# Attention inside a transformer layer: projections and value products cut in pieces and moved to other steps

## The reference, cut to what matters

```python
def diff_attention(q, k, v, lam):
    ...
    def block(qi):                     # 128 queries
        s = jnp.einsum('bqhtd,bkhtd->bhtqk', qi, k).astype(jnp.float32)
        p = jax.nn.softmax(s, axis=-1)
        a = p[:, :, 0] - lam * p[:, :, 1]
        return jnp.einsum('bhqk,bkhe->bqhe', a.astype(v.dtype), v)

h = rms_norm(x, g_pre_mix[l]) * (1.0 + sc1) + sh1
p = h @ w_in[l]
q, k, v, z, gates = jnp.split(p, SPLITS, axis=-1)
q = partial_rope(q.reshape(B, S, ATTN_HEADS, 2, ATTN_HEAD_DIM), cos, sin)
k = partial_rope(k.reshape(B, S, ATTN_HEADS, 2, ATTN_HEAD_DIM), cos, sin)
o = diff_attention(q, k, v, lam)
```

## Time and profile before

| | |
|---|---|
| median of three runs | 5690.43 us (5686.27 to 5692.12) |
| span of the profiled execution | 5687.6 us |
| PE busy / weight loads | 5157.5 us (91%) / 4000.4 us (70%) |
| DVE, ACT, POOL busy | 2979.1 (52%), 1455.1 (26%), 152.1 us (3%) |
| mean granted clock of TensorE | 0.905 of full speed |

### The profile page before, as it was taken

How to read it: one execution, slowest core, us unless ns; L and a number is a source line. 1 busy time by engine, 2 the same in 40 slices (tenths; PEclk the granted TensorE clock), 3 DMA queues, 4 the chain that set the end, 5 groups by cost and what they waited for, 6 DMA issues and landing times. The chain is left out here.

```text
span 5687.6 us, 59986 instructions
## 1 busy us (share of the span) xinstructions
PE 5157.5 (91%) x21520; PEld 4000.4 (70%) x21520; DVE 2979.1 (52%) x4767; ACT 1455.1 (26%) x1603; POOL 152.1 (3%) x96
## 2 busy tenths in 40 slices
PE   2999988869888789999999699999999999999997
PEld 2666655657666666666666478888888888888885
DVE  5676762145333685555555377744444444444445
ACT  3444442132212213333333211111111211111111
POOL 0000000010000000010001000000000000000000
PEclk9999987979898888788777699999999999999998
DMA  3000001134321101333333343422222222222212
GB/s 117 19 24 21 24 10 48 52 133 168 110 81 74 52 22 52 104 110 102 110 102 104 109 148 146 147 74 73 75 73 66 77 77 67 66 77 77 66 66 78
DMA packets 236046, 455.34 MB, mean 80 GB/s; under 512 B 12320, under 2 KB 143776, under 8 KB 232736
## 3 DMA queue, kind: packets, MB, share of 16 engines
q1 hardware_dynamic: 218656, 386.75, 20.4%
q10 hardware_dynamic: 11520, 37.75, 1.7%
q0 software_dynamic: 5760, 29.36, 1.5%
HBM read 336.38 MB, written 117.44 MB: 80 GB/s over the span
## 5 line engine op out<-in xcount | busy, mean ns | idle before, releaser
L2016 DVE TENSOR_TENSOR y<-y,psum 128x512 f32<-128x512 f32 x1024 | 680.4, 685 | 374.6 <-PE psum L375 374.4
L373 PE MATMUL psum<-act_hi,v_hi 128*128 128x512 f32 x2048 | 800.1, 391 | 55.2 <-DVE v_lo L1993 52.3
L374 PE MATMUL psum<-act_lo,v_hi 128*128 128x512 f32 x2048 | 798.8, 390 | 0.0
L375 PE MATMUL psum<-act_hi,v_lo 128*128 128x512 f32 x2048 | 798.6, 390 | 0.0
L373 PE MATMUL psum<-in_hi,u_hi 128*128 128x512 f32 x1408 | 548.0, 389 | 1.9 <-DVE u_lo L1982 1.9
L374 PE MATMUL psum<-in_lo,u_hi 128*128 128x512 f32 x1408 | 547.9, 389 | 0.0
L375 PE MATMUL psum<-in_hi,u_lo 128*128 128x512 f32 x1408 | 547.9, 389 | 0.0
L1986 DVE SCALAR_TENSOR_TENSOR g<-g,psum 128x1024 f32<-128x1024 f32 x88 | 107.5, 1222 | 769.9 <-ACT psum L1951 769.9
L373 PEld LDWEIGHTS psum<-act_hi,v_hi 128*128 128x128 f32 x2048 | 385.5, 188 | 139.9 <-issue 52.8
L1951 ACT ACTIVATE psum<-psum 128x1024 f32<-128x1024 f32 x88 | 88.7, 1008 | 1513.0 <-PE psum L375 1513.0
L375 PEld LDWEIGHTS psum<-act_hi,v_lo 128*128 128x128 f32 x2048 | 385.5, 188 | 80.3
(11 more groups left out here) (332 smaller groups left out, 8371.2 us busy)
## 6 DMA issues: line engine op xcount, KB each, us to landing
route_scratch<-sc_stage SPq DMA_DIRECT2D x32, 2048.0 KB, 10.7
g<-route_scratch SPq DMA_DIRECT2D x128, 512.0 KB, 3.3
v_raw<-peer_v_dram SPq DMA_DIRECT2D x128, 512.0 KB, 5.1
u_raw<-peer_uT_dram SPq DMA_DIRECT2D x88, 512.0 KB, 5.3
sc_u_raw<-peer_uT_dram SPq DMA_DIRECT2D x42, 512.0 KB, 5.3
hidden_scratch<-sc_gelu_t ACTq DMA_DIRECT2D x40, 512.0 KB, 6.2
u_raw<-hidden_scratch SPq DMA_DIRECT2D x40, 512.0 KB, 4.4
gates_ada<-w_adaT_dram POOLq DMA_DIRECT2D x16, 1024.0 KB, 5.7
```

The lines of the kernel that those rows point to most:

```text
L373: pe.matmul(out, w_hi, x_hi, start=start, stop=False)
L374: pe.matmul(out, w_hi, x_lo, start=False, stop=False)
L375: return pe.matmul(out, w_lo, x_hi, start=False, stop=stop)
L2016: dve.tensor_tensor(to, to, ps[:, 4 + n % 4], ALU.add).then_inc(added, 1)
```

## The change

Four things change in the attention's programs, and no instruction of the arithmetic is added or removed:

- `project` and `times_v` are returned as pieces; each step runs four eighths of its block of 24 matmuls ahead of `turn`, and four behind it.
- `PROJECTS` moves to steps 1, 2, 3, 5, 6, 7, `times_v(h, 1)` to step 0 of the next head. Each step of a head has now one block of 24.
- `scores` is called apart for map 0 and map 1, with `prepare` between them. `PREPARES` moves to steps 2, 3, 4, 6, 7, and the last value half (`LAST_V`) to step 0 of its own head. `SPLITS` moves to 0, 3, 6.
- ACT and DVE follow: in steps 0 and 4 `turned_hi` comes behind the exponentials, `out` behind it; on DVE `swing` or `low` of values comes ahead of `combine`. The first two and the last two heads are written out, the rest is the loop.

The diff, cut to its core: the loop and the tables, the bodies of ACT and DVE, then PE's program.

```diff
@@ -592,17 +595,20 @@
 
             def all_heads(eng, body, first=None):
 
-                with eng.Fori(0, HEADS // 2 - 1) as it:
+                body(None, Head(0, 0), Head(0, 1))
+                body(Head(0, 0), Head(0, 1), Head(0, 2))
+                with eng.Fori(1, HEADS // 2 - 1) as it:
                     for c2 in range(2):
-                        body(Head(it, c2), Head(it, c2 + 1))
+                        body(Head(it, c2 - 1), Head(it, c2), Head(it, c2 + 1))
                 last = HEADS // 2 - 1
-                body(Head(last, 0), Head(last, 1))
-                body(Head(last, 1), None)
-
-
-            PROJECTS = {b: b for b in range(6)}
-            PREPARES = {b: b - 1 for b in range(1, 7)}
-            SPLITS = {0: (QQ, 0), 2: (VV, 0), 4: (KK, 1)}
+                body(Head(last, -1), Head(last, 0), Head(last, 1))
+                body(Head(last, 0), Head(last, 1), None)
+            PROJECTS = {1: 0, 2: 1, 3: 2, 5: 3, 6: 4, 7: 5}
+            PREPARES = {2: 0, 3: 1, 4: 2, 6: 3, 7: 4}
+            LAST_V = 5
+            SPLITS = {0: (QQ, 0), 3: (VV, 0), 6: (KK, 1)}
 
...
-                    def body(h, g):
+                    def body(before, h, g):
                         for b in range(BPH):
                             e = PREPARES.get(b)
+                            if b == 0:
+                                high(h, LAST_V)
                             if g and e is not None and HALVES[e][0] == VV:
                                 high(g, e)
-                            turned_hi(h, b)
+                            if b % 4:
+                                turned_hi(h, b)
                             if b + 1 < BPH:
                                 exps(h, b + 1)
                             elif g:
                                 exps(g, 0)
+                            if b % 4 == 0:
+                                turned_hi(h, b)
+                                if b:
+                                    out(h, 0)
+                                elif before:
+                                    out(before, 1)
                             if g and b in SPLITS:
                                 i, after = SPLITS[b]
                                 if not after:
@@ -691,11 +707,8 @@
                                     split_weights(g.next(), i)
                             if g and e is not None and HALVES[e][0] != VV:
                                 high(g, e)
-                            if b == 4:
-                                out(h, 0)
                             if g and b in PROJECTS:
                                 copy(g, PROJECTS[b])
-                        out(h, 1)
...
-                    def body(h, g):
+                    def body(before, h, g):
                         for b in range(BPH):
-                            combine(h, b)
                             e = PREPARES.get(b) if g else None
+                            if b == 0:
+                                low(h, LAST_V)
                             if e is not None:
                                 if HALVES[e][0] == VV:
                                     low(g, e)
                                 else:
                                     swing(g, e)
+                            combine(h, b)
                             if b + 1 < BPH:
                                 maxima(h, b + 1)
...
-                        for k in range(KT):
+                        def piece(k):
                             last = self.product3(pe, job, w_hi[:, r, k], w_lo[:, r, k], h_hi[:, k, cols(half)], h_lo[:, k, cols(half)],
                                                  k == 0, k == KT - 1)
-                        last.then_inc(projected, 1)
+                            if k == KT - 1:
+                                last.then_inc(projected, 1)
+                        return piece
 
                     def prepare(g, e):
                         i, half = HALVES[e]
@@ -848,20 +869,22 @@
                             last = pe.matmul(job, self.rotate[:], plain[:, e % 2], start=True, stop=True)
                         last.then_inc(prepared, 1)
 
-                    def scores(h, b):
+                    def scores(h, b, m):
                         q = slice(b * P, (b + 1) * P)
-                        if b == 0:
+                        own = map_rows[m]
+                        if m == 0 and b == 0:
+                            pe.wait_ge(x_split, h.at(6, 9))
+                        if m == 0 and b == BPH // 2:
 
                             pe.wait_ge(x_split, h.at(6, 10))
-                        for m in range(2):
-                            own = map_rows[m]
-
-                            pe.wait_ge(exped, h.at(2 * BPH, 2 * b + m + 1))
-                            for half in range(2):
-                                to = ps[:, 2 * m + half]
-                                pe.matmul(to, q_twice[:, h.par, m, q], k_both[:, h.par, m, cols(half)], start=True, stop=False)
-                                last = pe.matmul(to, q_lo[own, h.par, q], k_both[own, h.par, m, cols(half)], start=False, stop=True)
-                            last.then_inc(scored, 1)
+                        pe.wait_ge(exped, h.at(2 * BPH, 2 * b + m + 1))
+                        for half in range(2):
+                            to = ps[:, 2 * m + half]
+                            pe.matmul(to, q_twice[:, h.par, m, q], k_both[:, h.par, m, cols(half)], start=True, stop=False)
+                            last = pe.matmul(to, q_lo[own, h.par, q], k_both[own, h.par, m, cols(half)], start=False, stop=True)
+                        last.then_inc(scored, 1)
 
...
-                        for k in range(TB):
+                        def piece(k):
                             v = slice(k * P, (k + 1) * P)
                             last = self.product3(pe, o_acc, v_hi[:, h.par, v], v_lo[:, h.par, v],
                                                  a_hi[:, k], a_lo[:, k], k == 0, k == TB - 1)
-                        last.then_inc(out_summed, 1)
-
-                    def body(h, g):
+                            if k == TB - 1:
+                                last.then_inc(out_summed, 1)
+                        return piece
+                    def body(before, h, g):
                         for b in range(BPH):
-                            if b + 1 < BPH:
-                                scores(h, b + 1)
-                            elif g:
-                                scores(g, 0)
+                            coming = (h, b + 1) if b + 1 < BPH else (g, 0) if g else None
+                            if coming:
+                                scores(*coming, 0)
+                            if b == 0:
+                                prepare(h, LAST_V)
                             if g and b in PREPARES:
                                 prepare(g, PREPARES[b])
+                            if coming:
+                                scores(*coming, 1)
+                            piece = None
                             if b == 4:
-                                times_v(h, 0)
+                                piece = times_v(h, 0)
+                            elif b == 0 and before:
+                                piece = times_v(before, 1)
+                            elif g and b in PROJECTS:
+                                piece = project(g, PROJECTS[b])
+                            for k in range(0, 4):
+                                if piece:
+                                    piece(k)
                             turn(h, b)
-                            if g and b in PROJECTS:
-                                project(g, PROJECTS[b])
-                            if b == BPH - 1:
-                                times_v(h, 1)
+                            for k in range(4, KT):
+                                if piece:
+                                    piece(k)
                     first = Head(0, 0)
                     for e in range(6):
-                        project(first, e)
-                        prepare(first, e)
-                    scores(first, 0)
+                        piece = project(first, e)
+                        for k in range(KT):
+                            piece(k)
+                        if e != LAST_V:
+                            prepare(first, e)
+                    for m in range(2):
+                        scores(first, 0, m)
                     all_heads(pe, body)
+                    piece = times_v(Head(HEADS // 2 - 1, 1), 1)
+                    for k in range(KT):
+                        piece(k)
 
```

More of the change, by code:

```diff
@@ L583, in next, with before @@
                     return Head(self.it, self.c + 1)
+                def before(self):
+                    return Head(self.it, self.c - 1)
                 def ring(self, i):
@@ L707, in _ @@
                             split_weights(first.next(), KK)
-                        high(first, e)
+                        if e != LAST_V:
```

(5 more changed lines are left out.)

## The result

The changed kernel is slower: a median of 5735.68 us over four runs (5729.82 to 5740.09) against 5688.35 (5680.82 to 5692.12) in four runs of the kernel before, a ratio of 1.008 with a 95% interval of 1.0066 to 1.0095. Forecast were 5755 us and a range of 5705 to 5795. The profiled span is 5728.2 us against 5687.6, 40.6 more.

A forecast was written before the change was run, and what follows sets the result against it. PE was taken to bound the kernel: 83.7 us of work, 12.9 of waits and 9.9 of clock a head. Seven heads make 745.5 against 668.8, +76.7, less 12 at the ends: 5755 us, range 5705 to 5795.

The forecast's parts named there:

- The chains of ACT and DVE: PE waits for ACT's and DVE's queues in steps 1, 3, 4, 5, 7: 1.6, 1.4, 2.1, 4.5, 3.3 us.
- The sum of the waits: PE's five new waits in each head together: 12.9 us.
- The work: PE's work in a head without any wait, including 0.7 us for divided blocks: 83.7 us.
- The clock: Slower PE clock after waits: 1.5 us for each of three short, 2.7 for each of two long; 9.9 a head.
- The ends: Outside the seven heads: 8 us less in head 0's step 0, 4 less in the last head; 12 less.
- The rival of the long waits only: Only PE's two long waits a head slow the clock, 5.4 us a head: +33, 5724 us; chance 0.12.
- The other side: PE's waits don't arise and blocks fill all eight steps: 83.7 us a head, 5595 us; chance 0.07.

The follow-up runs named there:

- experiment 1: Changed kernel with DVE taking combine of the next step ahead of turned_lo in steps 0 and 4: 5691.77 us, ratio 0.9998 to the kernel before.
- experiment 2: Changed kernel with ACT's copy of a projection ahead of split and high instead of behind them: 5691.56 us, ratio 0.9999 to the kernel before.
- experiment 4: Changed kernel with ACT's copy first, DVE's combine early and low of keys and queries later, value half 4 transposed into o_acc: 5580.0 us, ratio 0.9802.
- experiment 5: experiment 4 without the division: all eight pieces of a block stand behind turn; 5573.3 us, ratio 0.9804 to the kernel before.
- experiment 9: experiment 4 with ACT's copies of steps 2 and 3 last again, two short waits a step apart: 5646.39 us, ratio 0.992.
- experiment 8: experiment 4 with ACT's copy of step 2 alone last again, one short wait: 5609.98 us, ratio 0.9867 to the kernel before.
- experiment 7: experiment 4 with value half 4 back in job and low ahead of the maxima in step 7, one long wait: 5622.64 us, ratio 0.9892.
- experiment 3: Changed kernel without the division: all eight pieces of a block stand behind turn; 5842.89 us, ratio 1.0265 to the kernel before.
- experiment 10: experiment 3 with DVE taking combine ahead of swing and low of values: 5717.23 us, ratio 1.0044 to the kernel before.
- experiment 6: Changed kernel with the edits of experiment 1 and experiment 2 together: 5657.88 us, ratio 0.9952 to the kernel before.

## Why the prediction was right, and where its sizes were off

**The chains of ACT and DVE: right.** Predicted were five waits of 1.6, 1.4, 2.1, 4.5 and 3.3 us in steps 1, 3, 4, 5 and 7; measured are 0.7 to 1.1, 1.38, 1.89, 4.2 and 3.03. Experiments 1 and 2 show the two causes the steps named: the order on DVE for steps 1 and 5, the copy behind split and high on ACT for 3, 4 and 7. The queues were followed row by row, and in steps 3, 4, 5 and 7 the errors are 0.0 to 0.3 us.

**The sum of the waits: 12.9 forecast, 10.8 measured.** Step 1 was taken worst, 0.5 to 0.9 too long. Its chain counted 0.27 us from PE's start to ACT's; in step 5 it was 0.20 (626.15 to 626.35). PE also reached `turn` later, since scores and half a block took 6.32 us, not 6.08. That covers about 0.3 us; the rest of its error stays open. The errors of the other four steps add 0.8. The last part is step 5 in heads 2 and 5: there the trace has the clock low just before, PE came to `turn` later and waited 2.6 instead of 4.2. In experiment 2, where the clock is not low there, step 5 waits 4.2 us in all six heads. A low clock hides part of the next wait, and the sum had added both in full.

**The work: 83.7 forecast, 82.6 measured** (experiment 4). The term that was too large is the rotation, taken at 1.1 us: in experiment 5 a step takes 4.17 us from its first scores matmul to `turn` with a rotation and 3.31 without, 0.86 for each of the four.

**The clock: 9.9 us a head forecast, 8.5 measured**, the busy time of the six heads over that of experiment 4 (546.81 less 495.71, by six). That it came so near is partly luck, for the forecast's prices, 1.5 for a short wait and 2.7 for a long one, fail elsewhere: the two short waits of experiment 9 should cost 3.0 and cost 5.7, the three waits of experiment 1 should cost 5.7 and cost 9.1 (550.34 less 495.71, by six). By experiment 8 a short wait has an average price of 4/6 x 3.1 = 2.1. The five waits of the changed kernel come at 1.7 each, the two of experiment 9 at 2.8, the three of experiment 1 at 3.0. So no price per wait holds for all orders, and why five cost less than three was not tried. The clock fell more often than before, but not as often as the forecast said: 19 low stretches in the six heads, about three a head and not four or five, against 10 in the kernel before. From experiment 8, 12.29 us of extra busy time over 6 x 4.6 us of low clock, each us of low clock costs 0.45. With it, a head is 82.6 plus idle time plus 0.45 x low clock: 95.8 before (14.2 us low; measured 95.8), 101.6 after (measured 101.9), 98.0 in experiment 1 (98.4), 96.0 in experiment 2 (96.3). With the 3.04 us wait of experiment 7 it gives 0.5 too much, 89.1 for 88.6, and with the waits of 4 to 7 us in experiments 3 and 10 it gives 2.8 and 2.7 too much (from 82.0 of work: 122.3 for 119.5, 105.0 for 102.3). There part of the low stretch lies in the idle time, where it costs nothing: the clock is 0.84 in the wait of experiment 7 shown above, and 0.61 in the 7.13 us wait of the same head in experiment 10.

**The ends: 12 forecast, 11 measured** (6.6 and 4.5).

So the chain of waits held, and three terms were too large in the same direction: work by 1.1 us a head, waits by 2.1, clock by 1.4, in all 4.6 (106.5 forecast, 101.9 measured). They didn't cancel one another. Over the seven heads, head 0 being slower than the other six, it was 27.8 us (745.5 against 717.7). Forecast were +65, measured are +41 by the spans and +47 by the medians.

**The rival of the long waits only.** The Trainium skill (TensorE: Matmul & The Clock Gate, HAM oscillation) ties drops to long idle gaps. Taken so that 1.4 to 2.1 us pass free it does not hold here: 1.38 us alone had a drop in four of six heads. The total could not have told, since the 5724 us of this rival lie nearer to the measured 5736 than the forecast's 5755. A later section of the same page (A second HAM failure mode: psum-queue depth-cycling), which the prediction had not weighed, says of a kernel that goes round its PSUM banks in each iteration that short idle times between groups of matmuls, if frequent enough, make the clock swing too; in experiments 8 and 9 one and two short waits a head were enough for drops. The waits of 1.0 us and below that stand in experiments 2 and 6 beside longer ones were not tried alone; whether they ever lower the clock stays open.

**The other side.** The Trainium skill (Perfetto Trace Analysis, Optimization Strategy) says that interleaving stretches of different limits can help. Here it does once ACT and DVE are ordered for it: with every step of a head holding one block, experiments 4 and 5 leave 0.02 us of idle time a head and less and gain 2% (5580.0 us in experiment 4, where this rival had 5595). For this change it was put low, and it did not come. Its condition had two parts, waits below 8 us a head and a clock that holds. Experiment 1 met the first (6.7 us) and not the second, and came out no faster than the kernel before.

## What to carry to other kernels

When the pacing engine's blocks are spread evenly, walk each helper's queue in program order from the event that starts it to the one that the pacing engine asks for; each chain that had slack from a long block is now late by what the block lost. Put the instruction that the pacing engine asks for first ahead of any that waits for another engine (here `combine` ahead of `low`, `copy` ahead of `high`), and only then decide whether blocks need dividing: with the queues right, whole blocks did as well. Remove the waits to the last one, since a single wait of 1.4 us can cost 3.1 more in clock.

## What the runs showed of the hardware

- A wait with a drop to 1.2 GHz costs some 3.1 us of busy time, whether it was 1.38 or 3.04 us long (3.0 to 3.1 in four heads of experiment 8; 3.1 on average in experiment 7, 2.4 to 4.1 in single heads). What differs is how often it comes: in four heads of six for 1.38 us, in all six of experiment 7.
- Two waits of 1.38 and 1.89 us, a step apart, bring 12.5 us of low clock a head; one of 1.38 brings 4.6, one of 3.04 brings 8.0.
- The granted clock can fall inside a wait (0.84 in one of 3.04 us), and once more some 23 us after it, behind 17.00 us of fully busy PE (two heads of six, experiment 7).
- Less idle time need not mean a higher clock: 10.8 us a head with 18.2 us of low clock in the kernel after, 6.7 with 19.3 in experiment 1, 9.0 with 9.7 in experiment 2. Why the low stretches in experiment 1 lie as they do was not tried.
